# The inverse root of the heads' norms: from ACT and VectorE to a power on GpSimd, with the output taken a head later

## What is computed

```
o = diff_attention(q, k, v, lam, rel_bias)
o = rms_norm(o, subln_gain[l]) * (1 - lam_init)      # over the 128 columns of each head
y_attn = o.reshape(B, S, ATTN_W) @ w_attn_branch[l]
y_conv = conformer_conv(...)                         # conv, LayerNorm, silu, projection
merged = sigmoid(ga) * y_attn + sigmoid(gb) * y_conv
x = x + g2 * (merged @ w_mix_out[l])
```

## Time and profile before

| | us |
|---|---|
| median of three runs (2754.44 to 2755.12) | 2754.52 |
| the profiled execution: its own span | 2753.7 |
| PE busy in it | 2585.2 (94%) |
| DVE busy | 1748.2 (63%) |
| ACT busy | 1060.4 (39%) |
| POOL busy | 81.7 (3%) |

### The profile page before, as it was taken

How to read it: one execution, slowest core, us unless ns; L and a number is a source line. 1 busy time by engine, 2 the same in 40 slices (tenths; PEclk the granted TensorE clock), 3 DMA queues, 4 the chain that set the end, 5 groups by cost and what they waited for, 6 DMA issues and landing times.

```text
span 2753.7 us, 35127 instructions
## 1 busy us (share of the span) xinstructions
PE 2585.2 (94%) x11186; PEld 2030.9 (74%) x11186; DVE 1748.2 (63%) x2545; ACT 1060.4 (39%) x1497; POOL 81.7 (3%) x162
## 2 busy tenths in 40 slices
PE   4899998999999989999979999989999999899997
PEld 2688886776767767888858888867766678688886
DVE  3655567799998555543345556669999965655433
ACT  2433322444443434343234342244444443443422
POOL 0000010000000000000000001100000000000000
PEclk9999998999999999999989999989999999999998
DMA  5444474222222233433324446622222223343332
GB/s 221 142 149 142 151 224 142 81 76 72 80 80 84 84 114 115 152 122 95 97 83 145 153 129 208 211 66 79 76 73 83 77 87 122 101 143 107 97 92 93
DMA packets 472262, 320.39 MB, mean 116 GB/s; under 512 B 11303, under 2 KB 447785, under 8 KB 471176
## 3 DMA queue, kind: packets, MB, share of 16 engines
q1 hardware_dynamic: 445260, 227.69, 28.1%
q0 software_dynamic: 21888, 83.90, 8.9%
q10 hardware_dynamic: 5052, 8.02, 1.0%
HBM read 314.52 MB, written 5.05 MB: 116 GB/s over the span
## 4 chain that ended last, share of the span: by engine, by line
PE 68%; DVE 16%; issue 11%; ACT 3%; ACTq 1%; DVEq 1%
PE bank L1045 21%; PE bank L1047 21%; PE bank L1046 21%; DVE conv_part L858 5%; DVE rstd L616 3%; DVE w_lo L605 2%; ACTq L420 1%; ACT w_hi L377 1%; DVE probs L890 1%; PE bank L1063 1%; PE bank L1064 1%; PE bank L1065 1%; PE bank L1100 1%; DVE probs L906 1%; PE bank L1127 1%
## 5 line engine op out<-in xcount | busy, mean ns | idle before, releaser
L605 DVE TENSOR_TENSOR w_lo<-w_raw,w_hi 128x1024 fp32r<-128x1024 f32 (+1 forms) x434 | 522.6, 1205 | 721.5 <-ACT w_hi L377 720.6
L1046 PE MATMUL bank<-h_lo,w_hi 128*128 128x512 f32 x2336 | 911.3, 390 | 0.0
L1045 PE MATMUL bank<-h_hi,w_hi 128*128 128x512 f32 x2208 | 885.9, 401 | 17.9 <-DVE w_lo L605 17.8
L1047 PE MATMUL bank<-h_hi,w_lo 128*128 128x512 f32 x2208 | 862.9, 391 | 0.0
L377 ACT ACTIVATE w_hi<-w_raw 128x1024 fp32r<-128x1024 f32 (+1 forms) x434 | 452.4, 1043 | 912.8 <-PE bank L1047 893.1
L1045 PEld LDWEIGHTS bank<-h_hi,w_hi 128*128 128x128 f32 x2208 | 415.5, 188 | 134.9 <-issue 52.2
L1046 PEld LDWEIGHTS bank<-h_lo,w_hi 128*128 128x128 f32 x2336 | 440.1, 188 | 89.9 <-issue 3.8
L1047 PEld LDWEIGHTS bank<-h_hi,w_lo 128*128 128x128 f32 x2208 | 415.4, 188 | 89.0
L858 DVE SCALAR_TENSOR_TENSOR conv_part<-glu,conv_taps,conv_part 128x512 f32<-128x512 f32 x464 | 316.6, 747 | 0.0
L1045 PE MATMUL bank<-s_hi,w_hi 128*128 128x512 f32 x704 | 274.9, 390 | 0.0
L1047 PE MATMUL bank<-s_hi,w_lo 128*128 128x512 f32 x704 | 274.0, 389 | 0.0
(11 more groups left out here) (158 smaller groups left out, 2296.5 us busy)
## 6 DMA issues: line engine op xcount, KB each, us to landing
w_raw<-in_ffn_w_in SPq DMA_DIRECT2D x176, 512.0 KB, 3.8
ada_raw<-in_ada_w POOLq DMA_DIRECT2D x144, 512.0 KB, 4.7
w_raw<-in_w_mix_in SPq DMA_DIRECT2D x112, 512.0 KB, 3.7
w_raw<-in_ffn_w_out SPq DMA_DIRECT2D x64, 512.0 KB, 3.6
w_raw<-in_ffn_w_out SPq DMA_DIRECT2D x32, 384.0 KB, 3.1
w_raw<-in_w_mix_out SPq DMA_DIRECT2D x18, 512.0 KB, 3.6
ada_first<-in_ada_w POOLq DMA_DIRECT2D x8, 1024.0 KB, 24.4
w_raw<-in_w_attn_branch SPq DMA_DIRECT2D x16, 512.0 KB, 3.6
```

Of the source, the lines that this page charges most:

```text
L605: dve.tensor_tensor(wlo[slot][:, 0:n, :], raw[slot][:, 0:n, :], whi[slot][:, 0:n, :].bitcast(F32), ALU.subtract).then_inc(w_lo[slot], 1)
L1045: pe.matmul(acc, wh, hi[:, k0 + k, :], start=first and k == 0, stop=False)
L1046: pe.matmul(acc, wh, lo[:, k0 + k, :], start=False, stop=False)
L1047: mm = pe.matmul(acc, wl, hi[:, k0 + k, :], start=False, stop=last and k == n - 1)
```

## The change

The root becomes an affine ACTIVATE (`variance`: Identity, with the same scale and eps), and POOL raises RSTD to the power -1/2 in place, by a tensor_tensor whose second input is one column of -0.5, broadcast. DVE's reciprocal of the heads goes. In `mix` on DVE the gain moves from behind the second w_lo of the head to a place before `chains`, and unit_lo from behind scores(3) to behind z; on ACT unit_hi moves from behind V's copy to the end of the head. In the stage gb the same is done, with the taps around it regrouped. The three norms of the residual, the final one and the LayerNorm's keep root and reciprocal.

```diff
-RSN = 3 + HEADS + 1
+RSN = 4
 RS_NORM = (0, 1, RSN - 1)
-RS_HEAD, RS_VAR = 2, 2 + HEADS
+RS_VAR = 2
...
+    minus_half = at("minus_half", [P, 1], F32)
...
+        pool.memset(minus_half[:, :], -0.5).then_inc(sem("minus_half"), 1)
...
             with pool.Fori(0, CHUNKS_OUT) as g:
                 ada_chunk(l, g + (2 + CHUNKS_IN[0]), l * NMOD + CHUNK_SEQ["ffn1_out"] + g)
+            pool.wait_ge(sem("minus_half"), 1)
+            with pool.Fori(0, HEADS) as h:
+                pool.wait_ge(sem("aux_read"), l * AUXN + AUX_HEAD + 1 + h)
+                pool.tensor_tensor(RSTD[:, :], RSTD[:, :], minus_half[:, :].to_broadcast([P, TOK]), ALU.pow)\
+                    .then_inc(sem("head_rstd"), 1)
             with pool.Fori(0, CHUNKS_IN[1]) as g:
...
+        def variance(aux, unit):
+            act.wait_ge(sem("aux_ready"), aux + 1)
+            act.wait_ge(sem("unit_t"), unit)
+            act.activation(RSTD[:, :], AUX[:, :], ACT.Identity, bias=eps[:, 0:1], scale=float(D // P)).then_inc(sem("aux_read"), 1)
...
                     if not first:
-                        root(l * AUXN + AUX_HEAD + h - 1, l * UNITS + UNIT_HEAD + h - 1, float(D // P))
+                        variance(l * AUXN + AUX_HEAD + h - 1, l * UNITS + UNIT_HEAD + h - 1)
                     w_hi_part(p + 2, 0)
                     act.activation(VT[:, :], G[0][:, :], ACT.Copy).then_inc(acc_read[0], 1)
-                    if not first:
-                        unit_hi(l * UNITS + UNIT_HEAD + h - 1, 0, tile(AOHI2, h - 1))
                     exps(3)
...
                     act.activation(tile(GA2, h), G[1][:, :], ACT.Tanh, scale=0.5).then_inc(acc_read[1], 1)
+                    if not first:
+                        unit_hi(l * UNITS + UNIT_HEAD + h - 1, 0, tile(AOHI2, h - 1))
...
                         head_output(l * HEADS + HEADS - 1)
-                        root(l * AUXN + AUX_HEAD + HEADS - 1, l * UNITS + UNIT_HEAD + HEADS - 1, float(D // P))
+                        variance(l * AUXN + AUX_HEAD + HEADS - 1, l * UNITS + UNIT_HEAD + HEADS - 1)
...
-                    if j == 0:
+                    if j == 1:
                         unit_hi(l * UNITS + UNIT_HEAD + HEADS - 1, 0, AOHI[:, HEADS - 1, :])
...
                     w_lo_part(p + 1, 1)
-                    if not first:
-                        reciprocal(l * AUXN + AUX_HEAD + h - 1, l * RSN + RS_HEAD + h - 1)
-                        unit_gain(uh, 0, True, OT[:, :], subg[:, ds(l, 1)])
                     w_lo_part(p + 2, 0)
                     conv(17, 19)
                     dve.wait_ge(sem("bt_in"), (hh + 1) * 16)
                     scores(3)
-                    if not first:
-                        unit_lo(uh, 0, tile(AOLO2, h - 1), tile(AOHI2, h - 1))
...
                     combine(0)
                     if not first:
+                        dve.wait_ge(sem("head_rstd"), hh)
+                        unit_gain(uh, 0, True, OT[:, :], subg[:, ds(l, 1)])
                         chains(h - 1)
...
                                              op0=ALU.add, op1=ALU.mult).then_inc(sem("z_ready"), 1)
+                    if not first:
+                        unit_lo(uh, 0, tile(AOLO2, h - 1), tile(AOHI2, h - 1))
...
                     if j == 0:
                         uh = l * UNITS + UNIT_HEAD + HEADS - 1
-                        reciprocal(l * AUXN + AUX_HEAD + HEADS - 1, l * RSN + RS_HEAD + HEADS - 1)
+                        taps(HEADS - 1, 5, 13)
+                    if j == 1:
+                        dve.wait_ge(sem("head_rstd"), (l + 1) * HEADS)
                         unit_gain(uh, 0, True, OT[:, :], subg[:, ds(l, 1)])
-                        taps(HEADS - 1, 5, 8)
+                        taps(HEADS - 1, 22, DVE_TAPS)
                         unit_lo(uh, 0, AOLO[:, HEADS - 1, :], AOHI[:, HEADS - 1, :])
-                        taps(HEADS - 1, 8, 13)
-                    if j == 1:
-                        taps(HEADS - 1, 22, DVE_TAPS)
                         chains(HEADS - 1)
```

## The result

| | before | after |
|---|---|---|
| device time, median | 2754.82 us (4 runs) | 3642.4 us (4 runs) |
| ratio, 95% interval | | 1.3215 [1.3196, 1.3234] |
| span of the profiled execution | 2753.7 | 3640.7 |

The kernel is 888 us slower; 2722 was forecast, with 2800 as the upper end. The page after: busy times, the chain that ended last, and the groups that carry the difference; then the group of the taps in the page before.

The account below looks back on a forecast made before the run. DVE was taken to set the heads' pace, with PE nearly level. Gains of 11.1 us in the heads and 5.1 at the stage's end, 16.2 a layer, 32.4 in both, took 2754.5 to 2722; range 2710 to 2800.

Parts of the forecast that it names:

- the cover of the power: POOL's power runs hidden under 29 us of slack in the loop and about 16 at the stage's end; cost zero.
- P: Length of POOL's power on 128x512, in no row; taken as between 0.85 and 16 us.
- rival C: Power outlasts its cover: excess above 16 us paid at stage's end, above 29 in each head; 2844 at 35; chance 0.06.
- Rival B: DVE's two-input work in the heads is locked out while POOL's power runs, costing 16 P less 32.4 us; chance 0.28.
- The gain of the order: Mixing stage: 11.1 us from the heads and 5.1 at the end, 16.2 a layer, 32.4 in both.
- Steps 1 and 2: One head on DVE: reciprocal gone, scores(3) starts 2.4 us earlier; unit_lo moved too, scores(2) starts 2.73 us earlier.
- step 4: End of the mixing stage: reciprocal and its drain leave; PE's mean of the running sum comes 5.1 us earlier a layer.
- Under 0.7 us: On ACT, unit_hi behind GA's tanh delays the next w_hi by under 0.7 us, wanted only five taps later; costed at nothing.

Follow-up runs that it names:

- experiment 1: The changed kernel with POOL multiplying RSTD by 1e-10 instead of raising it to -1/2 (variance scale 0), same order and waits; 2734.06 us, ratio 0.992.
- experiment 7: The kernel before plus 100 POOL multiplies of 128x512 in each layer's heads, waited for by nobody; 2878.33 us, ratio 1.0443.

## Why the prediction was wrong

- **The step that failed** is the cover of the power: "Cost zero, between 0.85 and 16 us". No row bounded P from above; I took the reciprocal's 3.35 us as the nearest hard function and "several times that" as the end. It is 83.2 us. My sum for C with that P gives 2 x (83.2 - 16) + 14 x (83.2 - 29) - 32.4 = +861, so 3615, against 3642 measured. The mechanism of rival C was right; its P of 35 was far too short, its chance of 0.06 too small, and the range left it out.
- **The covers themselves** were right: 29 and 16 us forecast; the rows of experiment 1 give 29.5 in a head and 844.84 - 829.26 = 15.6 at the end (from the multiply's start to the gain there).
- **Rival B** was wrong for a power: the taps stay at 744 to 748 ns. DVE can be held up (experiment 7), but the holds seen are 0.8 us for an instruction of 512 columns, whether it lasts 1.04 us or 82.
- **The gain of the order**: 32.4 forecast, experiment 1 gives 24.7 by the traces: the last running sum comes 12.4 us sooner in the first layer, counted from the Z of head 0, (865.30 - 518.37) - (852.85 - 518.31), and 12.3 in the second. About 2 us come back between the layers, for a cause that I did not look for: the span is 23.0 us shorter (2753.7 and 2730.7). Steps 1 and 2 held (scores(3) 2.4 and scores(2) 2.7 us earlier from head 7's second w_lo), and step 4 as well: 5.2 against 5.1. Two terms were too large. A head gains 1.4, not 1.85, since DVE meets PE's transposes before scores(0) (0.32 us). And there are five steady heads, not six: the first of them starts from a head 0 without norm and taps, where PE is late, and DVE waits 2.85 us for w_hi instead of 0.83.
- **"Under 0.7 us"** for unit_hi on ACT was right only for a punctual gain. For a late one I had named PE's wait for the w_hi behind it; what PE waited for was the weights that ACT copies between the two.

The last running sums of the first layer, before and in experiment 1:

```profile
865.30 0.69 DVE L870 TENSOR_TENSOR running_sum<-running_sum,conv 128x512 f32<-128x512 f32 x1
...
852.85 0.69 DVE L883 TENSOR_TENSOR running_sum<-running_sum,conv 128x512 f32<-128x512 f32 x1
```

## What to carry to other kernels

An operation that no row of the trace shows on its engine has no upper bound by analogy with another engine's instruction: run it once beside the kernel, waited for by nobody, before building an order around it. Price it per column as well, since a value that is the same on all partitions can be turned onto them; here that makes 82.5 us into 1.0, or 4.3 in a head. Work on another engine is free only up to the length of its cover. Past it the excess is paid in full, and every engine stands that has work queued behind the waiting instruction: look there for what a late result stops.

## What the runs showed of the hardware

- A power on POOL costs 0.16 us a column and the same for 32 or 128 partitions; a multiply of the same shape takes 1.04 us for 512 columns.
- POOL's two-input instructions and DVE's hold each other up, DVE by about 0.8 us for each instruction of 512 columns on POOL (multiply or power) and by 0.14 for a power of 128. Among nine taps a single multiply waits 2.8 us and the taps lose nothing; a row of multiplies takes turns with them and doubles their time. What decides between the two was not found out.
- PE's granted clock falls while it waits and is low when it comes back: 0.54 in the 53.7 us of waiting, 0.50 in the 4.3 us after another such wait, 0.73 over the whole head, against 1.00 before.
